# Neighbourhood attention on one core: transposes three steps and values four steps behind the scores, with four score buffers

## The reference, cut to what matters

```python
s = einsum('...qngd,...knd->...ngqk', q, k) * HEAD_DIM ** -0.5
s = s + bias                      # latent keys: rpb by relative row and column; context keys: 0
s = where(mask, s, NEG_INF)       # the window of 16 columns
p = softmax(s, axis=-1)
o = einsum('...ngqk,...knd->...qngd', p, v)
```

## The kernel before, in words

| engine | iteration s |
|---|---|
| PE | score(s), turn(s-2), values(s-3), a part of turn_v |
| DVE | bias(s), take_latent of the last pair where b = 1, take_context where b = 3, probs(s-1) |
| ACT | exp(s), keep(s-2), a part of keep_v |

## Time and profile before

### The profile page before, as it was taken

How to read it: one execution, slowest core, us unless ns; L and a number is a source line. 1 busy time by engine, 2 the same in 40 slices (tenths; PEclk the granted TensorE clock), 3 DMA queues, 4 the chain that set the end, 5 groups by cost and what they waited for, 6 DMA issues and landing times.

```text
span 3120.5 us, 46692 instructions
## 1 busy us (share of the span) xinstructions
PE 2997.6 (96%) x16904; PEld 2404.8 (77%) x16904; DVE 1606.0 (51%) x2539; ACT 1147.7 (37%) x1755; POOL 1093.8 (35%) x506
## 2 busy tenths in 40 slices
PE   7999999999999999999998999999999999999999
PEld 5866787887857788877786687888888767778887
DVE  4447654455357554554317746541553347567272
ACT  3265441223274442222227733221232226543232
POOL 3433444443423444442232133222223330244443
PEclk9999999999999999999999999999999899999999
DMA  4431343443411343431110011221111110022223
GB/s 153 135 119 35 121 149 125 144 135 102 164 54 64 120 146 129 145 118 42 62 54 27 25 48 48 67 69 53 67 66 63 61 55 1 28 88 98 91 94 101
DMA packets 72795, 270.30 MB, mean 87 GB/s; under 512 B 7920, under 2 KB 8944, under 8 KB 72560
## 3 DMA queue, kind: packets, MB, share of 16 engines
q1 hardware_dynamic: 71024, 264.34, 25.6%
q10 hardware_dynamic: 1664, 4.51, 0.4%
HBM read 266.72 MB, written 2.10 MB: 86 GB/s over the span
## 4 chain that ended last, share of the span: by engine, by line
PE 57%; issue 27%; POOL 8%; DVE 5%; ACT 2%; POOLq 0%; DMA 0%; ACTq 0%; DVEq 0%
PE ps L665 43%; POOL w_lo L542 7%; PE ps L688 4%; PE ps L734 1%; DVE s_s L1987 1%; PE ps L845 1%; PE ps L834 1%; PE ps L1001 1%; PE ps L1019 1%; PE ps L980 1%; DVE s_s L1977 1%; PE ps L869 1%; PE ps L826 1%; DVE n_s L1924 1%; PE ps L729 1%
## 5 line engine op out<-in xcount | busy, mean ns | idle before, releaser
L542 POOL TENSOR_TENSOR w_lo<-w_raw,w_hi 128x1024 fp32r<-128x1024 f32 (+1 forms) x364 | 946.8, 2601 | 1527.8 <-ACT w_hi L1140 1527.8
L665 PE MATMUL ps<-h_hi,w_hi 128*128 128x512 f32 (+1 forms) x2832 | 954.7, 371 | 5.7 <-POOL w_lo L542 4.0
L665 PE MATMUL ps<-h_lo,w_hi 128*128 128x512 f32 (+1 forms) x2832 | 945.4, 368 | 0.0
L665 PE MATMUL ps<-h_hi,w_lo 128*128 128x512 f32 (+1 forms) x2832 | 944.2, 367 | 0.0
L1140 ACT ACTIVATE w_hi<-w_raw 128x1024 fp32r<-128x1024 f32 (+1 forms) x364 | 406.3, 1116 | 1357.1 <-PE ps L665 1230.1
L665 PEld LDWEIGHTS ps<-h_hi,w_hi 128*128 128x128 f32 x2832 | 490.4, 188 | 112.1 <-issue 8.4
L665 PEld LDWEIGHTS ps<-h_hi,w_lo 128*128 128x128 f32 x2832 | 490.2, 188 | 91.1
L665 PEld LDWEIGHTS ps<-h_lo,w_hi 128*128 128x128 f32 x2832 | 490.5, 188 | 88.7
L1767 DVE TENSOR_SCALAR conv_y<-u_pad,small 128x770 f32<-128x770 f32 (+1 forms) x88 | 174.7, 1985 | 192.5 <-ACT u_pad L1313 192.2
L1720 DVE SCALAR_TENSOR_TENSOR xT<-ps,mod,xT 128x512 f32 (+1 forms) x72 | 45.4, 658 | 307.6 <-PE ps L665 259.7
L1565 DVE CUSTOM_DVE_ANT_0 mod_junk<-mod_w,silu_c 128x1024 f32<-128x1024 f32 x96 | 137.6, 1433 | 113.8 <-DMA mod_w<-w_mod_dram 113.7
(11 more groups left out here) (213 smaller groups left out, 3750.4 us busy)
## 6 DMA issues: line engine op xcount, KB each, us to landing
mod_w<-w_mod_dram SPq DMA_DIRECT2D x96, 512.0 KB, 3.4
w_raw<-w_gu_dram SPq DMA_DIRECT2D x88, 512.0 KB, 3.3
w_raw<-w_down_dram SPq DMA_DIRECT2D x64, 704.0 KB, 4.0
w_raw<-w_up_dram SPq DMA_DIRECT2D x88, 512.0 KB, 3.3
w_raw<-w_in_dram SPq DMA_DIRECT2D x56, 512.0 KB, 3.3
w_raw<-na_qkv_dram SPq DMA_DIRECT2D x24, 512.0 KB, 3.3
w_raw<-w_out_dram SPq DMA_DIRECT2D x16, 512.0 KB, 3.3
w_raw<-swa_qkv_dram SPq DMA_DIRECT2D x12, 512.0 KB, 3.2
```

Source lines behind the costliest of these rows:

```text
L542: pool.tensor_tensor(w_lo[par][:, 0:cols], w_raw[par][:, 0:cols], w_hi[par][:, 0:cols].bitcast(F32), ALU.subtract).then_inc(w_lo_ready, 1)
L665: last = pe.matmul(acc[par][:, to:to + n], w[par][:, k * P:k * P + P], r[:, k, frm:frm + n], start=begin, stop=end)
```

## The change

The score buffers `n_s` go from three to four, and the statistics of a step (two extremes, two sums, two reciprocals) move from `stats` to `n_stat`, one set of six for each buffer, behind `n_s` in the same area. PE transposes step s-3 in iteration s where it transposed s-2, and computes the values of s-4 where it computed s-3. ACT keeps step s-3 in iteration s where it kept s-2. The parts of turn_v and keep_v move one iteration later, to b = 5, 0 and 1; take_latent moves from b = 1 to b = 2, and take_context from b = 3 to b = 4. DVE waits for `n_turned` of step s-4 before it writes a buffer. Each loop has one iteration more. Scores, bias, exponentials and probs stay where they were, and so do the two pairs of score banks and the two `n_pT`. No instruction of the 48 steps is added, removed or resized.

```diff
--- before.py
+++ after.py
@@ -353,7 +353,8 @@
         f_sq = [area(f"f_sq{i}", [P, S]) for i in range(2)]
         area = Area(h_at, h_size)
         n_vs = [area(f"n_vs{i}", [P, 9, P]) for i in range(2)]
-        n_s = [area(f"n_s{i}", [P, 2, S]) for i in range(3)]
+        n_s = [area(f"n_s{i}", [P, 2, S]) for i in range(4)]
+        n_stat = area("n_stat", [P, 4, 6])
         n_pT = [area(f"n_pT{i}", [P, 2, S]) for i in range(2)]
         n_bias = at(temp_at, [P, 2, 3, S], name="n_bias")
         area = Area(mask0_at, 2 * nbytes([P, STRIP]))
@@ -998,7 +999,7 @@
                         pe.wait_ge(n_kept, s)
                     for hd in range(2):
                         for c in range(4 if s % 6 < 4 else 2):
-                            last = pe.transpose(bank(hd)[:, c * P:c * P + P], n_s[s % 3][:, hd, c * P:c * P + P],
+                            last = pe.transpose(bank(hd)[:, c * P:c * P + P], n_s[s % 4][:, hd, c * P:c * P + P],
                                                 mat(IDENT))
                     last.then_inc(n_turned, 1)
 
@@ -1022,18 +1023,18 @@
                                 last.then_inc(n_values, 1)
 
                 pe.wait_ge(acc_free, ph["unit0"])
-                for s in range(48 + 3):
+                for s in range(48 + 4):
                     j, b = divmod(s, 6)
                     if s < 48:
                         score(s)
                     if j == 0 and b < 3:
                         turn_v(0, b)
-                    if 2 <= s < 50:
-                        turn(s - 2)
-                    if s >= 3:
-                        values(s - 3)
-                    if s >= 4 and (s - 4) % 6 < 3 and (s + 2) // 6 < 8:
-                        turn_v((s + 2) // 6, (s - 4) % 6)
+                    if 3 <= s < 51:
+                        turn(s - 3)
+                    if s >= 4:
+                        values(s - 4)
+                    if s >= 5 and (s - 5) % 6 < 3 and (s + 1) // 6 < 8:
+                        turn_v((s + 1) // 6, (s - 5) % 6)
 
             def swa(ph):
                 pe.wait_ge(acc_free, ph["unit0"])
@@ -1418,9 +1419,9 @@
                     w = S if s % 6 < 4 else C
                     for hd in range(2):
                         act.wait_ge(n_biased, 2 * s + hd + 1)
-                        act.activation(n_s[s % 3][:, hd, 0:w], n_s[s % 3][:, hd, 0:w], ACT.Exp,
-                                       bias=stats[:, 6 * (s % 3) + hd:6 * (s % 3) + hd + 1], scale=-1.0,
-                                       accum_out=stats[:, 6 * (s % 3) + 2 + hd:6 * (s % 3) + 3 + hd]).then_inc(n_exped, 1)
+                        act.activation(n_s[s % 4][:, hd, 0:w], n_s[s % 4][:, hd, 0:w], ACT.Exp,
+                                       bias=n_stat[:, s % 4, hd:hd + 1], scale=-1.0,
+                                       accum_out=n_stat[:, s % 4, 2 + hd:3 + hd]).then_inc(n_exped, 1)
 
                 def keep(s):
                     w = S if s % 6 < 4 else C
@@ -1432,16 +1433,16 @@
                                    ).then_inc(n_kept, 1)
 
                 act.activation(stats[:, 21:22], eps1[:], ACT.Exp)
-                for s in range(48 + 2):
+                for s in range(48 + 3):
                     j, b = divmod(s, 6)
                     if s < 48:
                         exp(s)
                     if j == 0 and b < 3:
                         keep_v(0, b)
-                    if s >= 2:
-                        keep(s - 2)
-                    if s >= 4 and (s - 4) % 6 < 3 and (s + 2) // 6 < 8:
-                        keep_v((s + 2) // 6, (s - 4) % 6)
+                    if s >= 3:
+                        keep(s - 3)
+                    if s >= 5 and (s - 5) % 6 < 3 and (s + 1) // 6 < 8:
+                        keep_v((s + 1) // 6, (s - 5) % 6)
 
             def swa(ph):
                 act.wait_ge(hn_out, ph["hn0"])
@@ -1906,22 +1907,21 @@
                     if b < 4:
                         dve.wait_ge(n_table, 6 * j + 2 * MASK_KIND[b] + 2)
                     dve.wait_ge(n_scored, 2 * s + 2)
-                    if s >= 3:
-                        dve.wait_ge(n_turned, s - 2)
+                    if s >= 4:
+                        dve.wait_ge(n_turned, s - 3)
                     dve.memset(pace[:, s % 4:s % 4 + 1], 0.0)
                     for hd in range(2):
                         table = n_bias[:, hd, MASK_KIND[b], :] if b < 4 else n_bias[:, 0, 0, 2 * P:4 * P]
-                        at_ = 6 * (s % 3) + hd
-                        dve.tensor_tensor_reduce(n_s[s % 3][:, hd, 0:w], bank(4 + 2 * (s % 2) + hd, w), table, -1.0, -NEG,
-                                                 ALU.add, ALU.min, stats[:, at_:at_ + 1]).then_inc(n_biased, 1)
+                        dve.tensor_tensor_reduce(n_s[s % 4][:, hd, 0:w], bank(4 + 2 * (s % 2) + hd, w), table, -1.0, -NEG,
+                                                 ALU.add, ALU.min, n_stat[:, s % 4, hd:hd + 1]).then_inc(n_biased, 1)
 
                 def probs(s):
-                    w, at_ = S if s % 6 < 4 else C, 6 * (s % 3)
+                    w = S if s % 6 < 4 else C
                     dve.wait_ge(n_exped, 2 * s + 2)
-                    dve.reciprocal(stats[:, at_ + 4:at_ + 6], stats[:, at_ + 2:at_ + 4]).then_inc(n_recip2, 1)
+                    dve.reciprocal(n_stat[:, s % 4, 4:6], n_stat[:, s % 4, 2:4]).then_inc(n_recip2, 1)
                     dve.wait_ge(n_recip2, s + 1)
                     for hd in range(2):
-                        dve.tensor_scalar(n_s[s % 3][:, hd, 0:w], n_s[s % 3][:, hd, 0:w], stats[:, at_ + 4 + hd:at_ + 5 + hd],
+                        dve.tensor_scalar(n_s[s % 4][:, hd, 0:w], n_s[s % 4][:, hd, 0:w], n_stat[:, s % 4, 4 + hd:5 + hd],
                                           None, ALU.mult).then_inc(n_probs, 1)
 
                 def take_latent(j):
@@ -1933,13 +1933,13 @@
                     dve.wait_ge(n_values, 12 * j + 12)
                     dve.tensor_copy(proj[:, j, S:T2], bank(3, C)).then_inc(n_taken, 1)
 
-                for s in range(48 + 4):
+                for s in range(48 + 5):
                     j, b = divmod(s, 6)
                     if s < 48:
                         bias(s)
-                    if j and b == 1:
+                    if j and b == 2:
                         take_latent(j - 1)
-                    if j and b == 3:
+                    if j and b == 4:
                         take_context(j - 1)
                     if 1 <= s <= 48:
                         probs(s - 1)
```

## The result

The changed kernel takes 3131.51 us (median of 15 runs, 3128.47 to 3135.06) against 3124.04 us before (15 runs, 3121.80 to 3128.60). The ratio is 1.0020 with a 95% interval of 1.0012 to 1.0027: the change costs about 6 us, 4 to 8; the two medians lie 7.5 us apart. The forecast was 3128.0 in a range from 3121 to 3132, "within 0.2%". The direction holds, and so does the mechanism in all but the first pair.

What follows compares the result with a forecast made beforehand. No engine is full; PE waits 2.1 us a middle pair, and ACT's keep behind exp still holds turn. First pair -0.6, six middle pairs +1.9, last pair +2.9: +4.2 on 3123.82 gives 3128.0 us, range 3121 to 3132.

Steps and rivals of the forecast that it cites:

- the mechanism: In ACT's queue, keep(s-4) runs behind exp(s-1), so turn(s-3) still waits and a fourth buffer does not help.
- the first pair: From first scores to the second pair: turn(1) waits for keep(0), then 5.31 us of PE work; 0.6 us less.
- What bounds it: No engine is full; PE's own work is 17.48 us of a 19.55 us middle pair, leaving 2.1 us of waits.
- a second condition stood 0.1 us behind the first: At PE's turn: DVE's scaled scores are the named releaser, but ACT's keep ended only 0.1 us sooner.
- The chain of a middle pair: bias(2), take_latent, slowed scaling, bias(3), keep(0), turn(1), then 5.31 us of PE work: 19.87 us against 19.55, 0.32 more.
- The scaling behind take_latent: DVE's pair of scalings after the copy, beside POOL's table: 1.29 us assumed, bounds 0.81 and 1.77.
- The price of POOL's company: POOL running beside DVE's scalings was taken to cost them 0.5 to 0.6 us per us of company.
- The last pair: From its first scores to the last copy: one more turn and values behind the last scores, 25.4 us against 22.55, 2.9 more.
- the granted clock should stay at 1.00: Sign expected in the profile after the change: TensorE's clock stays at its full level.
- The waits of L1001 should name ACT: Sign in the profile: PE's waits before transposes name ACT's n_pT for nearly all, 15 to 20 us, DVE almost none.
- The slower rival: take_latent beside POOL's tables makes scaling cost its full 1.77 us: pair 20.35, sum +7.1, whole 3131; chance 0.18.

## Why the prediction was right, and where it was off

**What bounds it** held. PE's own 17.48 us a pair was measured at 17.52 once nothing held it. That a second condition stood 0.1 us behind the first was the step that decided the case, and the pair of runs with `keep` first shows it from both sides.

**The chain of a middle pair** held, step by step: 19.87 worked out, 19.96 in the common pair. The scaling behind take_latent took 1.39 us of DVE's queue (1671.16 to 1672.55) for the 1.29 assumed, between its bounds of 0.81 and 1.77, and those 0.1 us are the rest of the difference. That the mean change is 0.32 for a forecast of 0.32 is luck: the common pair went from 19.55 to 19.96, 0.41 more, and the means agree because one pair was longer before (19.92) and two were shorter after (19.85 and 19.86).

**The price of POOL's company was read wrongly.** The prediction set aside the rule of the Trainium skill, "SBUF — State Buffer", section "Who interferes with whom", that the one of the two engines that has the shared ports keeps them for its whole instruction and the other is fully blocked. It did so because the earlier trace rows took 1.45 us and the rule, as it was worked out, 2.04. But a row with x2 is two instructions, and the rule is for one. The same rows one by one:

```profile
1711.64 0.74 POOL L557 TENSOR_TENSOR n_bias<-n_rpb,n_mask 128x256 f32<-128x256 f32 x1 [1.60 <-DVE stats L1915]
1712.01 0.65 DVE L1924 TENSOR_SCALAR n_s<-n_s,stats 128x512 f32<-128x512 f32 x1
1712.32 0.92 POOL L557 TENSOR_TENSOR n_bias<-n_rpb,n_mask 128x256 f32<-128x256 f32 x1
1712.58 0.95 DVE L1924 TENSOR_SCALAR n_s<-n_s,stats 128x512 f32<-128x512 f32 x1
```

Undisturbed, such a scaling takes 0.49 us and such an instruction of POOL 0.73. Here they take turns: the first scaling ends 0.28 us behind POOL's first, POOL's second 0.58 behind that scaling, the second scaling 0.28 behind POOL's second. In the stage of the kernel before, 29 scalings of 512 columns that ran beside POOL ended so, 0.28 to 0.31 us behind an instruction of POOL. Taken one instruction at a time the trace agrees with the page, and "POOL costs it 0.5 to 0.6 us a us of company" is no rate at all, nor would the rule have made the pair 0.3 us longer. The 1.39 us behind take_latent, one by one:

```profile
1670.53 0.73 POOL L558 TENSOR_TENSOR n_bias<-n_rpb,n_mask 128x256 f32<-128x256 f32 x1 [5.10 <-DVE n_stat L1915]
1671.16 1.06 DVE L1924 TENSOR_SCALAR n_s<-n_s,n_stat 128x512 f32<-128x512 f32 x1
1671.22 0.73 POOL L558 TENSOR_TENSOR n_bias<-n_rpb,n_mask 128x256 f32<-128x256 f32 x1
1672.15 0.47 DVE L1924 TENSOR_SCALAR n_s<-n_s,n_stat 128x512 f32<-128x512 f32 x1
```

This time POOL's second instruction went ahead of the first scaling, which again ends 0.28 us behind it (1671.95 and 1672.23), and the second scaling ran undisturbed. That the assumed 1.29 came near was the narrow bounds' doing. Which of the two goes first when both stand ready is not settled by these rows: the scaling's record starts 0.06 us sooner, and POOL went ahead.

**The last pair** held to 0.02 us, and its steps to 0.1: one more turn and one more values stand behind the last scores, with ACT and PE taking turns. The kernel with five buffers, one step further, pays another 2.3 us there.

**The first pair failed.** The step was "Then keep(0) at +2.16, turn(1) at +1.15, and 5.31 of work". The starts were right; the 5.31 us of work were priced at the clock of a pair without long idleness, though the same chain said that PE would stand for 3.5 us there. They took 6.8 us, the first 3.2 of them at the lower level, so "the granted clock should stay at 1.00" was wrong as well. That is 1.5 us, all by which the stage exceeded its forecast (5.7 for 4.2), and most of the about 2 us by which the forecast of the whole was low.

**The test in the profile failed too.** "The waits of L1001 should name ACT" was sound on who releases and wrong on who is named. Read as it was written, the test would have thrown out a theory that was true. The quantity in it, 15 to 20 us of waits, was right (19.1).

**The slower rival**, the scaling at its full 1.77, did not occur. The case lies at its edge for another reason.

## What to carry to other kernels

When a wait is to be removed by more distance, list every condition of the waiting instruction and follow each back through the **queue** of the engine that fulfils it: here a copy that was three steps old stood behind the newest exponentials, so that neither a fourth buffer nor a fifth freed it; putting it ahead of them turned a change that lost 6 us into one that wins 14. Two edits can each be worth nothing and be worth much together, so where two conditions end within 0.1 us of each other try both at once. And a releaser's name in a profile is a guess when two engines end together: check it against the value that the wait asks for.

## What the runs showed of the hardware that was not expected

After a single idle stretch of 3.5 us, in another run of 2.5 and in another of 2.3, the granted clock fell to 0.50 in a stage that otherwise ran at 1.00, and the price came on the work behind it: 1.94 us for transposes of 1.09. With 0.5 us left of the stretch the clock stayed.

DVE's scalings and POOL's additions in SBUF shut each other out one instruction at a time, and a merged row of two hides it: 0.28 us from the end of POOL's instruction to the end of the scaling that stood behind it, against 0.49 for an undisturbed one.

The same matmul stream ran at two speeds with the clock granted in full. Busy time by stretch in the projections behind the stage, first of the kernel before, then of the kernel after (us, and in brackets the count of records):

```profile
1990.00:2070.00 80.00, 80.00 (x463) 69.96 (x462) 47.64 (x39) 23.71 (x37) 23.97 (x10) 1.00 0.22 69
```

```profile
1997.00:2079.00 82.00, 82.00 (x466) 71.14 (x465) 47.71 (x40) 24.17 (x38) 24.27 (x10) 1.00 0.21 68
```

Read from start to start, 100 PE records take 17.33 us in the one and 17.67 in the other, for some 900 to 1,000 records, about 3 us in all. It is not the kernel: the changed one with the gap filled by 26 transposes and the changed one with the copies later ran at 17.33, the one before with four buffers and with `keep` first at 17.67, and one and the same kernel, the changed one with `keep` first, at 17.33 in one execution and 17.66 in the other. What sets it is open; no run was made for it. It is not the only thing that varies: those two executions of one kernel both took 3111.57 us; the one at 17.33 had begun the stage 1.6 us later and lost the rest elsewhere. Over the 13 profiles the stage begins between 1641.3 and 1645.9 us, with the same program ahead of it. A difference of one profiled execution to another below some 5 us in this program has to be read stage by stage.
